# A hybrid decoder layer on one core: the input projection's q, k, v and conv tiles as three fp32r products, and the first sequence's K pages scored by heads

## What is computed

```
p = rmsnorm(h, norm_w) @ w_in                 # 1024 x 9232
qkv_a, z, a, b, q, k, v, gate_a, gate_b = split(p)
# branch A: causal conv (4 taps) over qkv_a, then a chunked gated delta rule (5 chunks)
# branch B: stick-breaking attention of the prompt (8 heads of 128), and for the samples:
kp = cache_k[page_table]                      # 8 sequences x 16 pages x 128 keys x 8 heads x 128
z  = einsum(q, kp) * SB_SCALE + bias          # one query per sequence and head
h += (sigmoid(gate_a) * (o_a @ w_pa) + sigmoid(gate_b) * (o_b @ w_pb)) @ w_o
h += (silu(x @ w_g) * (x @ w_u)) @ w_out      # then the final rmsnorm
```

## Time and profile before

| | |
|---|---|
| median of 3 runs | 1641.56 us (1638.34 to 1643.76) |
| the profiled execution | 1639.83 us, span 1638.1 us |
| PE busy | 1496.4 us, 91% of the span |
| DVE, ACT, POOL busy | 751.4, 503.7, 139.4 us |
| mean granted TensorE clock | 0.934 |
| moved by DMA | 253 MB, mean 154 GB/s |

### The profile page before, as it was taken

One profiled execution on the slowest core, in us unless ns is written; L12 is line 12 of the kernel. 1 busy time (PEld: TensorE's weight loads), 2 busy tenths in 40 slices (PEclk: granted clock), 3 DMA queues, 4 the chain that ended last, 5 costly groups with the idle time before them and its releaser, 6 DMA issues.

```text
span 1638.1 us, 26196 instructions
## 1 busy us (share of the span) xinstructions
PE 1496.4 (91%) x9866; PEld 1303.6 (80%) x9866; DVE 751.4 (46%) x2955; ACT 503.7 (31%) x725; POOL 139.4 (9%) x228
## 2 busy tenths in 40 slices
PE   6999897778999988896999899999889999999997
PEld 4777775556778778895877677889879999999996
DVE  2018745997986855654133221225343333332223
ACT  3011015652574322342122434222233222322122
POOL 0000001111221033210041000000000000000000
PEclk9999898998999997787799899999899999999998
DMA  3249873667774420001979998964122333332321
GB/s 108 64 120 329 263 240 137 202 193 242 235 231 138 123 75 7 8 1 30 284 255 329 341 313 262 324 206 143 52 65 78 95 98 91 90 91 81 97 81 52
DMA packets 238754, 252.98 MB, mean 154 GB/s; under 512 B 22361, under 2 KB 197603, under 8 KB 238597
## 3 DMA queue, kind: packets, MB, share of 16 engines
q1 hardware_dynamic: 238629, 251.31, 48.1%
HBM read 236.18 MB, written 15.29 MB: 154 GB/s over the span
## 4 chain that ended last, share of the span: by engine, by line
PE 73%; DVE 13%; DMA 4%; ACT 4%; issue 2%; POOL 2%; SPq 1%; POOLq 0%; DVEq 0%; ACTq 0%
PE ps L883 39%; PE ps L864 14%; DVE kring L1811 5%; PE ps L912 4%; DMA kring<-in_cache_k 3%; PE ps L965 2%; PE ps L848 2%; PE ps L1244 1%; PE ps L1144 1%; PE ps L976 1%; PE ps L938 1%; PE ps L1263 1%; PE ps L1161 1%; PE ps L1134 1%; PE ps L836 1%
## 5 line engine op out<-in xcount | busy, mean ns | idle before, releaser
L864 PE MATMUL ps<-xn,wring 128*128 128x268 f32 (+2 forms) x1568 | 363.7, 393 | 5.3 <-DVE xn L1794 4.4
L864 PEld LDWEIGHTS ps<-xn,wring 128*128 128x128 f32 (+1 forms) x1568 | 296.8, 190 | 69.6 <-issue 13.2
L1811 DVE CUSTOM_DVE_ANT_0 kring<-kring,qv 128x128 f32<-128x128 f32 x1024 | 231.9, 294 | 46.4 <-DMA kring<-in_cache_k 46.2
L1403 ACT ACTIVATE R<-ps 128x520 f32<-128x520 f32 (+1 forms) x86 | 52.4, 610 | 450.8 <-PE ps L864 237.6
L494 DVE TENSOR_TENSOR wring_split<-wring,vring_split 128x1024 fp32r<-128x1024 f32 (+1 forms) x76 | 90.8, 1195 | 204.0 <-ACT vring_split L487 204.0
L883 PE MATMUL ps<-xn_split,vring_split 128*128 128x260 f32 x704 | 142.2, 283 | 7.6 <-DVE obT_split L508 7.6
L883 PE MATMUL ps<-obT_split,vring_split 128*128 128x260 f32 x704 | 142.8, 284 | 0.0
L883 PE MATMUL ps<-xn_split,wring_split 128*128 128x260 f32 x704 | 142.0, 283 | 0.0
L487 ACT ACTIVATE vring_split<-wring 128x1024 fp32r<-128x1024 f32 (+1 forms) x76 | 78.5, 1034 | 171.0 <-DMA wring<-in_w_ffn_out 102.9
L883 PEld LDWEIGHTS ps<-xn_split,vring_split 128*128 128x128 f32 x704 | 109.1, 190 | 8.2 <-issue 7.6
L883 PE MATMUL ps<-R_split,vring_split 128*128 128x260 f32 x592 | 111.3, 285 | 2.3 <-DVE rows_split L508 2.3
(11 more groups left out here) (371 smaller groups left out, 2223.7 us busy)
## 6 DMA issues: line engine op xcount, KB each, us to landing
kring<-in_cache_k SPq DMA_DIRECT2D x128, 512.0 KB, 4.7
wring<-in_w_in SPq DMA_DIRECT2D x72, 512.0 KB, 5.2
vring<-in_cache_v SPq DMA_DIRECT2D x64, 512.0 KB, 5.5
kring<-in_cache_v SPq DMA_DIRECT2D x64, 512.0 KB, 5.4
wring<-in_w_ffn_in SPq DMA_DIRECT2D x44, 512.0 KB, 3.8
wring<-in_w_ffn_out SPq DMA_DIRECT2D x16, 512.0 KB, 3.8
qv<-qdram SPq DMA_DIRECT2D x8, 512.0 KB, 5.7
out_rec_sample<-R SPq DMA_DIRECT2D x4, 1024.0 KB, 10.1
```

What stands on the lines that cost most here:

```text
L864: last = mm(ps[0:m, 2 * (t % 2) + i, 0:n], w_block(p, kk), src[:, k, a + i * n:a + i * n + n], start=(k == 0), stop=(k == n_k - 1))
L1403: go(halves(dst[:, first_token(t):TOKENS]), pair(t, m), func).then_inc(act_read, 1)
L1811: m = v.tensor_tensor_reduce(kh, kh, qbc[:, b % 2, h * P:h * P + P], 1.0, 0.0, ALU.mult, ALU.add, dz[:, b % 4, p * H + h:p * H + h + 1])
```

## The change

- `tile` is gone. Tiles 0 to 48 go through `tile_split`, with all 536 tokens or the last 520 as before. The normalised input is split once, right where it is made, instead of in the chunk stage.
- The pieces 0 to 48 are now split too, by `split_hi` and `split_lo`; SPLIT_AT says at which tile's place in the lists of ACT and DVE a piece is split: piece t + 1 at tile t up to tile 10, piece t + 2 at tiles 11 to 42, t + 1 again after that.
- The high parts lie in buffers that are free then (vacc, two slots of vring), and a split waits until its buffer's last tile is done.
- The first sequence's 16 K pages are loaded at the start, into kring, vring and parts of R. They are scored by heads (`first_head`): for head h a matrix with that head's query on the diagonal (`diagonal`, DVE) is multiplied by ones (`spread_head`, PE), ACT copies the result into the query row (`row_of`), and DVE scores that head for all 16 pages.
- K_PLAN has 18 pages in s = 0 instead of 32, 44 in the attention instead of 40, 17, 13 and 4 in s = 2 to 4 instead of 20, 14 and 6. The ring has 6 slots until the end of attention, then 4.
- The decays of branch A are worked out during the q tiles. On SP a weight piece is asked for ahead of the K pages of its tile from s = 2 on. The clearing of two inverse buffers on POOL (`zero_inverse`) moves from conv tile 1 to conv tile 22.

```diff
+def split_lead(t):
+    return 2 if 11 <= t <= 42 else 1
+for _p in range(2, T_Z):
+    SPLIT_AT.setdefault(min(t for t in range(T_Z) if t + split_lead(t) >= _p), []).append(_p)
...
-K_PLAN = [((0, q), 8) for q in range(4)] + [((1, q), 4) for q in range(4)]
-K_PLAN += [(("att", i), 3 - i % 2) for i in range(2 * H)]
+K_PLAN = list(zip([(0, q) for q in range(4)], (4, 5, 5, 4))) + [((1, q), 4) for q in range(4)]
+K_PLAN += [(("att", i), 3 - (i % 4 == 3)) for i in range(2 * H)]
...
 # SP
-            for p in range(T_SEG + 3):
+            for p in range(RING):
                 w_load(sp, p)
...
+            for p in range(PAGES):
+                if p == PAGES - 2:
+                    sp.wait_ge(par_t, 2)
+                page_into(k_view(p), 0, p).then_inc(k_first, 16)
+            for p in range(RING, T_SEG + 3):
+                w_load(sp, p)
+            for i in range(2):
+                for b, p in K_ISSUE[-1, KT - 2 + i]:
+                    k_page(b, p)
...
 # PE
+            def spread_head(h):
+                pe.wait_ge(q_diag, h + 1)
+                if h >= 2:
+                    pe.wait_ge(q_row, h - 1)
+                mm(ps[:, 6 + h % 2, 0:P], ones[:, :], diag[h % 2][:, :], start=True, stop=True).then_inc(q_mm, 1)
             for t in range(T_SEG):
-                tile(t, xn, t == 0)
+                tile_split(t, n_hi, n_lo, None if t else 0, first_token(t), g_lo)
+                if t == 2:
+                    decay_rows()
+                    pe.wait_ge(cb_c, 2)
+                if t >= 2:
+                    spread_head(t - 2)
...
 # ACT
+            def row_of(h):
+                act.wait_ge(q_mm, h + 1)
+                nc.scalar.copy(qbc[:, 0, h * P:h * P + P], ps[:, 6 + h % 2, 0:P]).then_inc(q_row, 1)
+            splits(T_AB)
             read_tile(T_AB, abT[:, :], m=2 * H)
             for n in range(KT):
+                splits(T_Q + n)
                 read_tile(T_Q + n, qbT[:, n, :])
-            decays()
+                if n >= 2:
+                    row_of(n - 2)
+                if n == 4:
+                    decays()
...
 # DVE
+            def first_head(h):
+                dve.wait_ge(q_row, h + 1)
+                for p in range(PAGES):
+                    kh = k_view(p)[:, h * P:h * P + P]
+                    m = v.tensor_tensor_reduce(kh, kh, qbc[:, 0, h * P:h * P + P], 1.0, 0.0, ALU.mult,
+                                               ALU.add, dz[:, 0, p * H + h:p * H + h + 1])
+                    if h == H - 1:
+                        m.then_inc(k_used, 1)
+            splits(T_AB)
+            for h in range(H):
+                splits(T_Q + h)
+                diagonal(h)
+                if h == 0:
+                    dve.wait_ge(k_first, 16 * PAGES)
+                if h >= 1:
+                    first_head(h - 1)
+                if h == 2:
+                    decays()
+                if h == 5:
+                    log_decays()
+            splits(T_SEG)
+            first_head(H - 1)
+            scale_scores(0)
+            splits(T_SEG + 1)
             dve.wait_ge(qr_t, 1)
             v.tensor_copy(qrow[:, :].rearrange("p (a n) -> p a n", a=2), ps[0:DB, 6:8, :]).then_inc(qr_c, 1)
-            decays()
-            log_decays()
```

More of the change, by code:

```diff
@@ L137, with k_slot, k_use, k_before @@
     _n += _count
+K_LATE = PAGES + sum(_count for _key, _count in K_PLAN if _key[0] in (0, 1, "att"))
+def k_slot(n):
+    if n < PAGES:
+        return n
+    return (n - PAGES) % 6 if n < K_LATE else (n - K_LATE) % RING
+def k_use(n):
+    return sum(k_slot(m) == k_slot(n) for m in range(PAGES, n + 1))
+def k_before(n):
+    return max((m for m in range(n) if k_slot(m) == k_slot(n)), default=None)
 K_ISSUE = {}
@@ L850, in square_sums, with tile_split @@
                     m.then_inc(sq_used, 1)
[L852 to L869 removed]
+            def tile_split(t, hi, lo, ready=None, a=0, arrived=None):
                 if t >= 2:
@@ L1635, in _ @@
                         exp_decays()
+                    if t == 11:
+                        act.wait_ge(k_used, PAGES)
+                    if s == 2 and j == 5:
+                        act.wait_ge(k_used, K_LATE)
+                    if s == 3 and j == 0:
+                        act.wait_ge(ob_out, 16)
+                    if s < 5:
+                        splits(t)
                     if (s, j) in SOFT_AT:
@@ L1641, in _ @@
                         read_tile(t, (kbT, vbT)[s][:, j, :])
+                        if s == 0 and j < 2:
+                            row_of(H - 2 + j)
                     elif s in (2, 3, 4):
@@ L2113, in chunks @@
                         levels(c + 1)
-                    if 1 <= c <= 3:
-                        if c == 1:
-                            dve.wait_ge(w_used, done(T_SEG + 5 * KT - 1))
-                        for k in range(3 * c - 3, min(3 * c, KT)):
-                            gate_lo(dve, k, n_hi[k], n_full[k], n_lo[k])
             def sampled_delta():
@@ L2178, in _ @@
             dve.wait_ge(xt_d, KT)
+            split_lo(dve, 0)
+            split_lo(dve, 1)
             normalise(0, hT0, 0, rstd)
@@ L2199, in _ @@
                 for q in range(4):
+                    t0 = T_SEG + s * KT + 2 * q
+                    if (s, q) != (0, 0):
+                        splits(t0)
                     if (s, q) in SP_AT:
@@ L2208, in _ @@
                         conv((s - 2) * KT + 2 * q - 2)
+                        if s < 4:
+                            splits(t0 + 1)
                         conv((s - 2) * KT + 2 * q - 1)
-                    for b, p in K_PAGES.get((s, q), []):
+                    pages = K_PAGES.get((s, q), [])
+                    for i, (b, p) in enumerate(pages):
+                        if i == 2 and s < 2 and (s, q) != (0, 0):
+                            splits(t0 + 1)
                         k_page(b, p)
+                    if (s, q) == (2, 0) or s == 4:
+                        splits(t0 + 1)
                     if (s, q) == (3, 3):
```

195 lines of the change are left out of this document (106 added, 89 removed).

## The result

| | before | changed |
|---|---|---|
| device time, median (lowest to highest) | 1641.76 us (1638.34 to 1643.76) | 1705.93 us (1703.37 to 1708.48) |
| span of the profiled execution | 1638.1 us | 1706.8 us |
| mean granted clock of TensorE | 0.934 | 0.909 |

The changed kernel is slower: ratio 1.0393, 95% interval 1.0369 to 1.0417. That is 64 us more, where 27 were forecast, and above the forecast's range, which ended at 1692.

The account below looks back on a forecast made before the run. It took the DVE and ACT list order, holding PE up at the q tiles, as deciding, and DVE as having little room in s = 2 to 4. Terms +34 + 3 - 9 - 1 = +27 us on 1641.6 gave 1668 us, range 1641 to 1692.

Parts of the forecast that it names:

- Start: Tiles 0 to 3: input split ahead of normalising costs 1.2 us; tile 0 ends near 49.5, tile 3 near 68.1.
- Chain at the query tiles: Ahead of tiles 4 to 11: reading, row, DVE's scores and low part follow serially, 5.9 us of idle PE each.
- The clock's price: Slower PE clock after each pause at the q tiles: 2.5 us a pause, bounds nothing and 4.4 us.
- Rival (1): Pauses at the q tiles too short to lower PE's clock: 22 us less, 1646 us; chance 0.15.
- From tile 10 to attention: Tile 10's end to tile 12's start 21.3 us, then PE-bound tiles 84.1 us; attention at 277.4, 34 us behind.
- nothing else takes its place: Tiles 12 to 24: the old 8.98 us PE stall behind K pages goes and no other wait replaces it.
- Attention: Four extra pages in attention, three costing 1.08 us each: 3 us more, bounds 0 and 8.
- s = 2 to 4: Conv stages: PE would save 27 us, DVE's added splits limit the gain to 9 us; bounds 27 and -3.
- DVE's pace is PE's: s = 2: reading conv tiles waits for DVE's taps, so at most 2 us of gain there.
- Above 90% busy: Sign expected in s = 2: DVE above 90% busy and the stage no shorter than 68 us.
- Chunks and the rest: Chunk stage: eight input splits, done beside PE's work, go; 1 us less, bounds 0 and 5.
- Rival (4): Half clock for whole tiles adds 17 us; with attention +8 and no gain in s = 2 to 4, 1700; chance 0.12.

Follow-up runs that it names:

- q_ahead: Changed kernel with, at the q tiles, DVE's low part of the next weight piece ahead of the scores of head h - 1: 1656.9 us, ratio 1.0091.
- w_first: q_ahead's and conv_order's edits plus tile 12's piece split earlier; on top, more weights asked for ahead of pages, their low parts earlier: 1636.4 us.
- plan: w_first with the K pages of s = 0 and 1 dealt out later, none ahead of the query row's round through DRAM: 1636.7 us.
- conv_order: Changed kernel with a pair's odd low part behind the second K page, not between the two convolutions, in s = 2 and 3: 1686.8 us.
- arg_first: q_ahead's and conv_order's edits, tile 12's piece split earlier, and the subtraction of cumulative sums ahead of the pages in two pairs: 1624.8 us.
- arg_alone: Changed kernel with only DVE's subtraction of the cumulative sums moved ahead of the K pages in two conv pairs: 1697.2 us, ratio 1.0345.
- fp32_order: Changed kernel with conv tiles of s = 2 to 4 back to fp32, splits cut to 8 columns, plus conv_order's edit: 1679.7 us, ratio 1.0234.

## Why the prediction was wrong

- **Start.** Forecast: tile 0 ends near 49.5, tile 3 at 68.1. Their readings began at 50.33 and 68.27. Right.
- **Chain at the query tiles.** The step that I called deciding was right: a gap of 5.9 us forecast, 5.38 to 6.03 measured ahead of tiles 4 to 10, and 5.9 again ahead of tile 11 with the transposes in it, by the links named. q_ahead removed it ahead of tiles 4 to 10. The clock's price was 1.9 us a pause, not 2.5, so a period was 13.6 us instead of 14.4, and tile 10 ended at 163.6 instead of 170.4. Rival (1), clock kept, fell: 0.53 in the window 76 to 78. The Trainium skill ("TensorE: Matmul & The Clock Gate", What's actually happening) puts the penalty of the clock's ramp under 1% of a typical kernel's span. The seven pauses stay under that, and matter all the same: they cost 13 us, 0.8% of the span of 1706.8 us, but 14% of the 95 us between the readings of tiles 3 and 10.
- **From tile 10 to attention.** The start of attention was forecast at 277.4 and measured at 277.57, but that is luck: three errors cancelled. Tile 10 ended 6.8 us early. The way from there to tile 12 took 24.2 us, not 21.3, because the second sequence's query row took 9.1 us from its store's issue to its first page's product, where I had 5.5. And from the start of tile 12 (187.83) to attention it was 89.7 us, not 84.1 + 1.6. PE was busy 85.1 us of these, so taking it as the bound was near enough here, but "nothing else takes its place" was wrong: at 218.87 PE waited 3.12 us for the running sums. With an earlier start the waits for pages and running sums grow, and no order in w_first or plan took them away.
- **Attention.** 3 us more forecast, 2.7 measured.
- **s = 2 to 4.** The step that failed. Forecast was a gain of 9 us, with bounds of a gain of 27 and a loss of 3; measured was a loss of 34. I summed busy times (DVE gets 4.4 us more on 67.1 in 71.7) and wrote "DVE's pace is PE's". DVE's volume was forecast well: 16 us more in the three stages, 13 measured against the earlier trace rows. But it was busy only 62.1 of 88.2 us in s = 2; not its volume but the order of its list was at fault. What I had done at the query tiles, following list against list to see which entry waits for which, I didn't do here, where the change had put a low part between two convolutions. conv_order gives 20.2 us for that place. The second knot gives 10.5 to 13.9 us (arg_first, arg_alone); in the old kernel its waits were 1.99 and 0.48 us. The loop isn't what holds it open: without it, in conv_order, PE's waits for the logarithms fall only from 21.6 to 17.2 us. In fp32_order, with fp32 products and hardly any splitting in these stages, they are 6.0 us; which part of the change opens it no run shows. All edits together leave 204.1 us against 200.0 before. PE's own saving was overrated too: its busy time there fell from 206.2 to 190.7 us, 15.5 instead of 27, at a clock of 0.88 to 0.93 instead of 1.00. "Above 90% busy" as a sign of s = 2 was wrong for the same reason as the sum.
- **Chunks and the rest.** 1 us less forecast, 2.6 measured.
- **Sum.** 34 + 3 - 9 - 1 = 27 forecast, 34.3 + 2.7 + 34.3 - 2.6 = 68.7 on the profiled execution. The difference is nearly all one term, s = 2 to 4. Rival (4), 1700, was nearest in number, but by a mechanism that didn't occur: at the query tiles the half clock lasted 4 us of a tile's 8, not the whole tile.

## What to carry to other kernels

Before summing busy times in a stage, walk the in-order lists of two engines against each other around every entry that a change inserts: an operation that waits for the other engine, put between two that the other engine waits for, closes a loop, and its price is the whole turn. Look also for waits that are small today and stand behind a long stretch of other work: here 1.99 and 0.48 us became 8.81 and 7.58. A measured gap can be moved for nothing: check whether the work that has to pass through the stretch, here 34 pages after a late query row, allows an earlier end before the waits are reordered.

## What the runs showed of the hardware

Over seven pauses in a row, each of 5.4 to 6.0 us, a pause cost about 1.9 us of half clock, with one small matmul (L1334) right before each pause and none in it. In q_ahead PE kept a clock of 1.00 from 68 to 113 us through one pause of 0.28 and one of 1.48 us. In s = 2 to 4 the kernel with less PE work ran at a lower mean clock: 0.92 with PE busy 188 of 221.5 us (conv_order) against 0.98 with 209 of 217 (fp32_order). So part of the time saved on products was lost again on slower ones.
